# A two-layer decoder step on one core: expert rows scattered to token order, empty slots skipped, other order of the first loads

## The reference, cut to what matters

```
g_idx = argmax(g_logits)                       # one of 4 groups
top_v, top_i = top_k(e_sel, 2)                 # two of its 8 experts
up = t @ w_up[g];  gate, val = split(up)       # 1024 -> 2 x 256
hid = silu(gate) * val * comb
out = out + hid @ w_down[g]                    # 256 -> 1024
x = layer_norm(alpha * x + out)
```

## Time and profile before

| | |
|---|---|
| median of 3 runs | 1686.9 us (1682.15 to 1692.32) |
| profiled execution, its own time | 1689.43 us |
| its span, first to last instruction | 1687.8 us |
| PE busy | 1314.4 us, 78% of the span |
| DVE, ACT, POOL busy | 29%, 24%, 7% |
| granted TensorE clock, mean | 0.849 |
| DMA | 340.30 MB, mean 202 GB/s |

### The profile page before, as it was taken

The page is one execution under the profiler, slowest core; times in us unless marked ns, Lnnn a source line. Parts: engine busy times, 40 slices in busy tenths (PEclk is TensorE's granted clock), DMA queues, the critical chain, the costliest instruction groups (busy, mean ns, idle before and its releaser), DMA issues.

```text
span 1687.8 us, 17971 instructions
## 1 busy us (share of the span) xinstructions
PE 1314.4 (78%) x7094; PEld 899.7 (53%) x7094; DVE 493.2 (29%) x989; ACT 398.0 (24%) x757; POOL 121.5 (7%) x146
## 2 busy tenths in 40 slices
PE   7979997688667877772799999997688496787840
PEld 6979995556432322222799978783466332232310
DVE  2353137544510000006410157314443400000007
ACT  3112221530112222221212146322420022122110
POOL 0200001000000000005200020000000000000013
PEclk9989998698778988885897969797788698898875
DMA  8532214500579999975114040142400879999953
GB/s 317 225 112 75 88 38 140 186 7 32 201 269 414 414 414 415 413 287 192 41 39 155 26 151 1 38 132 87 124 25 25 338 272 414 414 413 415 413 194 109
DMA packets 161794, 340.30 MB, mean 202 GB/s; under 512 B 18610, under 2 KB 53570, under 8 KB 161474
## 3 DMA queue, kind: packets, MB, share of 16 engines
q1 hardware_dynamic: 143698, 274.98, 43.4%
q0 software_dynamic: 13424, 47.65, 7.5%
q10 hardware_dynamic: 4608, 16.78, 2.4%
HBM read 299.57 MB, written 39.81 MB: 201 GB/s over the span
## 4 chain that ended last, share of the span: by engine, by line
PE 55%; DMA 19%; DVE 11%; SPq 9%; ACT 4%; issue 2%; POOL 0%; ACTq 0%; DVEq 0%
DMA weight_ring<-in_w_up_dram 9%; PE ps L671 8%; PE ps L672 8%; PE ps L673 8%; PE ps L860 8%; DMA expert_weights<-in_w_up_dram 6%; SPq L444 6%; SPq L448 3%; PE ps L1132 2%; PE ps L924 2%; PE ps L1154 2%; PE ps L792 2%; PE ps L1200 1%; DVE small L1716 1%; DVE x_rows L1724 1%
## 5 line engine op out<-in xcount | busy, mean ns | idle before, releaser
L860 PE MATMUL ps<-weight_ring,work 128*64 128x512 f32 x512 | 139.5, 706 | 62.0 <-DMA weight_ring<-in_w_up_dram 62.0
L1855 DVE TENSOR_TENSOR work<-ps,work 128x256 f32<-128x256 f32 x32 | 13.6, 424 | 519.3 <-ACT work L1390 519.3
L860 PE MATMUL ps<-expert_weights,work 128*64 128x512 f32 x512 | 135.8, 691 | 34.8 <-DMA expert_weights<-in_w_up_dram 32.3
L860 PEld LDWEIGHTS ps<-weight_ring,work 128*64 128x64 f32 x512 | 47.4, 163 | 153.6 <-issue 153.6
L672 PE MATMUL ps<-weight_ring_r,mix_cols_r 128*128 128x384 f32 (+3 forms) x360 | 121.4, 338 | 0.0
L860 PEld LDWEIGHTS ps<-expert_weights,work 128*64 128x64 f32 x512 | 41.8, 159 | 127.4 <-issue 84.0
L673 PE MATMUL ps<-mix_cols_r,weight_ring_r 128*128 128x272 f32 x352 | 102.4, 291 | 0.0
L1390 ACT ACTIVATE work<-ps 128x256 f32<-128x256 f32 x32 | 12.3, 383 | 260.3 <-PE ps L860 260.3
L546 POOL DMA_INDIRECT work<-stream_rows,ints x34 | 32.0, 943 | 540.4 <-PE ps L841 493.3
L672 PEld LDWEIGHTS ps<-weight_ring_r,mix_cols_r 128*128 128x128 f32 (+1 forms) x360 | 67.4, 187 | 4.2
L671 PE MATMUL ps<-expert_weights_r 128*128 128x512 f32 (+1 forms) x160 | 68.5, 428 | 0.4 <-DVE mix_cols_r L1708 0.4
(11 more groups left out here) (365 smaller groups left out, 2443.5 us busy)
## 6 DMA issues: line engine op xcount, KB each, us to landing
expert_weights<-in_w_up_dram SPq DMA_DIRECT2D x32, 2048.0 KB, 19.8
weight_ring<-in_w_up_dram SPq DMA_DIRECT2D x32, 2048.0 KB, 19.8
expert_weights<-in_w_down_dram SPq DMA_DIRECT2D x32, 1024.0 KB, 16.7
mix_cols<-in_w_down_dram SPq DMA_DIRECT2D x32, 1024.0 KB, 16.0
expert_rows<-work ACTq DMA_DIRECT2D x32, 512.0 KB, 6.6
weight_ring<-in_w_in_a_dram SPq DMA_DIRECT2D x8, 1536.0 KB, 6.5
expert_rows<-expert_weights POOLq DMA_DIRECT2D x16, 512.0 KB, 9.9
weight_ring<-in_w_o_dram SPq DMA_DIRECT2D x4, 2048.0 KB, 13.0
```

What stands on the lines that cost most here:

```text
L860: last = mm(bank(0, rows=(t.start, t.stop)), xgT[:, k, t], WU[2 * q + j][:, k, :], start=(k == 0), stop=(k == KD - 1))
```

## The change

1. **Slots.** Constants `token` and the new `target` are stored minus 4096 (`FAR`); DVE adds 4096 to both lists. A filled slot gets its token and its row `token + 544 j` in the new layout of `expert_rows` (two halves of 544 rows); an empty one gets 4096, which the bounds of gather and scatter leave out. `bb` grows from 64 to 96 columns.
2. **Gather and scatter.** Both are indirect DMAs with a bounds check, issued by POOL. The scatter takes the place of the copy issued by ACT, and stands in POOL's order between two gathers. ACT's loop over pairs is written out.
3. **Combination.** SP loads a tile's two rows by one plain DMA; POOL only adds. In layer 0 `chunk(CH_S)` stands after the rows of tile 0, `chunk(CH_S + 1)` after those of tile 1.
4. **No zero fill** of `expert_rows`, and no wait for it.
5. **First loads.** SP loads input rows, weight chunk 0 and the rotary tables ahead of the other memory chunks; PE forms memory chunks 1 to 3 after heads 2, 5 and 8.
6. Some semaphores are merged into `f_step` and `fs_step`, with the same order of work.

```diff
-        ys_all = nc.dram_tensor("expert_rows", [(PAIRS + MORE) * P, D], F32, kind="Internal").ap()
+        ys = nc.dram_tensor("expert_rows", [2 * TOK, D], F32, kind="Internal").ap()
...
+            def gather(l, tokens, landed):
+                pool.indirect_dma_start(xg, None, xs[l], bass.IndirectOffsetOnAxis(tokens, 0), bounds_check=TOK - 1,
+                                        oob_is_err=False).then_inc(landed, 16)
+
+            def scatter(rows, landed):
+                pool.indirect_dma_start(ys, bass.IndirectOffsetOnAxis(rows, 0), yb, None, bounds_check=2 * TOK - 1,
+                                        oob_is_err=False).then_inc(landed, 16)
...
-                for i in range(PAIRS + 1):
-                    pool.wait_ge(S("xg_free"), b + i + 1)
-                    pool.indirect_dma_start(xg, None, xs[l], bass.IndirectOffsetOnAxis(slot_tok[:, i:i + 1], 0)) \
-                        .then_inc(S("xg_in"), 16)
+                gather(l, slot_tok[:, 0:1], S("xg_in"))
+                for i in range(PAIRS):
+                    pool.wait_ge(S("xg_free"), b + i + 2)
+                    gather(l, slot_tok[:, i + 1:i + 2], S("xg_in"))
+                    pool.wait_ge(S("y_ev"), s + i + 2)
+                    scatter(slot_to[:, i:i + 1], S("y_out"))
...
+            def expert_rows(l, i):
+                if i == 0:
+                    sp.wait_ge(S("y_out"), 16 * PAIRS * (l + 1))
+                    sp.wait_ge(S("rows_done"), l + 1)
+                if i >= 2:
+                    sp.wait_ge(S("yg_used"), NT * l + i - 1)
+                n = ROWS[i]
+                sp.dma_start(yg[i % 2][0:n], ys.rearrange("(j t) d -> t j d", j=2)[P * i:P * i + n]) \
+                    .then_inc(S(f"yg_in{i % 2}"), 16)
...
-                    last = mm(bank(5, 0, 64), a1[:, n, :], bb[:, n, :], start=(n == 0), stop=(n == 9))
+                    last = mm(bank(5, 0, 3 * NE), a1[:, n, :], bb[:, n, :], start=(n == 0), stop=(n == 9))
...
+                if h in (2, 5, 8):
+                    mem_kv_chunk((h + 1) // 3)
             pe.wait_ge(S("mkv_ev"), 8)
+            for l in range(LAYERS):
+                mem_keys_columns(l)
+            pe.wait_ge(S("mkt_ev"), 2)
```

More of the change, by code:

```diff
@@ L327, in build @@
         a1 = view(work, 2530, 10, P)
-        bb = view(work, 3810, 10, 2 * NE)
+        bb = view(work, 3810, 10, 3 * NE)
         esw = view(work, 6976, NT * NG * EG)
@@ L503, in _ @@
             experts(0)
-            sp.wait_ge(S("yg_in0"), 32)
-            for n in range(CH_S, CH_END):
+            expert_rows(0, 0)
+            chunk(CH_S)
+            expert_rows(0, 1)
+            chunk(CH_S + 1)
+            for i in range(2, NT):
+                expert_rows(0, i)
+            for n in range(CH_S + 2, CH_END):
                 chunk(n)
-            sp.wait_ge(S("tables"), 64)
+            sp.wait_ge(S("tables"), 48)
             sp.wait_ge(S("fm_mm"), 10)
@@ L526, in _ @@
             experts(1)
+            for i in range(2):
+                expert_rows(1, i)
+            for i in range(2, NT):
+                expert_rows(1, i)
             for i in range(ST):
@@ L581, in _ @@
-            nc.gpsimd.memset(zeros, 0.0).then_inc(S("pool_zero"), 1)
-            pool.wait_ge(S("pool_zero"), 1)
-            pool.wait_ge(S("rope_mm"), 1)
-            for b in range(MORE):
-                pool.dma_start(ys_all[(PAIRS + b) * P:(PAIRS + b + 1) * P], zeros).then_inc(S("zero_out"), 16)
+                pool.sem_inc(S("rows_done"), 1)
+                for i in range(NT):
+                    pool.wait_ge(S(f"yg_in{i % 2}"), 16 * ((3 if i % 2 == 0 else 2) * l + i // 2 + 1))
+                    y = yg[i % 2][0:ROWS[i]]
+                    nc.gpsimd.tensor_tensor(y[:, 0], y[:, 0], y[:, 1], ALU.add).then_inc(S("yg_sum"), 1)
```

207 lines of the change are left out of this document (98 added, 109 removed).

## The result

The changed kernel takes 1710.2 us (median of 4 runs, 1706.2 to 1716.8), the kernel before 1687.8 (4 runs): a ratio of 1.014, 95% interval 1.010 to 1.018. It is slower by 22 us; the forecast was 1657 and faster. The profiled execution is the longest of the four, 1716.81 us, its span 1715.1.

A forecast was written before the change was run, and what follows sets the result against it. Bytes were taken to bound the expert stages, PE and its DVE/ACT feeders the rest. Terms -20.4, -1.4, +1.2, -5.4, -1.4, -2.6 sum to -30.0 us: 1659.4, or 1657 against the median; 8 in 10 within 1642 to 1679.

The forecast's parts named there:

- The pace of bytes: Expert stages: all DMA engines busy at 414 GB/s, so transfers set the time of a pair, 17.6 us.
- the large term: Expert stages: skipping empty slots saves 2.3 rows a transfer on the fullest engine, 10.2 us a layer, -20.4 us (0 to -33).
- the even end: Expert stages: empty rows spread evenly over engines, 3.75 rows saved a transfer, 16.6 us a layer; as a rival 1644 us, 21%.
- the sign that should tell: Expert stages: DMA share stays near 1.04 if all engines lose rows, falls below 1 if the fullest sets the pace.
- Scatter on POOL between gathers: Expert stages: POOL waits for a pair's copied result and scatters before issuing the next gather; cost 0.
- the right ring: Expert stages: up product's end to result 7.3 us, scatter and gap, gather landing 6.9 us; 15.4 us in all.
- Its cover: Expert stages: turning wants the gather at about 16.9 us, leaving 1.5 us spare, then PE's wait for weights, about 3 us.
- The rival on the slower side: Expert stages: POOL becomes the bound if scatter and gather each take 5 us; about 1713 us, 6% with the like.
- Start: Before the experts: no zero fill delays chunk 2, less low clock, some new waits; -5.4 us (-12 to +2).
- Routing: Ahead of the first gather in both layers: a third part of `bb` and one more list; +1.2 us (0 to +2.5).
- First gather: Start of each expert stage: fewer rows per engine land it sooner; -1.4 us in both layers (0 to -6).
- Combination: After the experts: scatter and plain load replace copy and gathers; -1.4 us in layer 1, -2.6 in layer 0.

The follow-up runs named there:

- e3: The kernel before, plus a wait on POOL for pair i's copied result before the gather of pair i+2; 1688.2 us, ratio 0.999.
- e4: The kernel before, with only the gathers skipping empty slots (bounds check, `xg` zeroed once a layer), copies unchanged; 1674.1 us, ratio 0.991.
- e8: The kernel before, with the sixteen zero fills issued later, after the first projected rows of the second phase; 1676.9 us, ratio 0.992.
- e1: The changed kernel, with POOL issuing the gather of pair i+2 before the wait for pair i's result and the scatter; 1674.0 us, ratio 0.991.
- e6: The changed kernel with the gather issued ahead of wait and scatter, and no row skipped; 1698.0 us, ratio 1.005.
- e5: e1 with the slots of an expert dealt evenly over the partitions; 1665.3 us, ratio 0.982.
- e9: e5, without zero fill, with first loads and memory products in the order of the kernel before; 1654.9 us, ratio 0.981.
- e10: e6, but the scatter writes the pair's own block of rows, one behind the other; 1695.4 us, ratio 1.004.
- e14: e10 with a plain DMA issued by POOL in place of the indirect scatter; 1698.3 us, ratio 1.005.
- e2: The changed kernel, order on POOL kept, but no row skipped: empty slots move real or spare rows; 1742.2 us, ratio 1.031.

## Why the prediction was wrong

**The pace of bytes and the large term: right.** Bytes set the pace before (e3, e4, e8 keep the waits for weights). The term was 10.2 us a layer, 2.3 rows a transfer. Read alone (e1 against e6) it is 10.7 and 13.0, 2.4 and 2.9 rows. Dealt evenly (e5 against e6) it is 16.4 and 16.3, the even end of 16.6. The figure worked out from the Trainium skill, "DMA: Bandwidth & Descriptors", section "The descriptor swizzle", was 15.5 for both layers; 23.7 were measured, so these transfers save more than it gives. The pair of 17.0 us did not come all the same: behind the two short intervals e1's pairs take 17.8 and 17.6 us, those of the kernel before 17.8, since the copy's new queue (below) takes back what the rows give. What was wrong is the sign that should tell: the DMA share stayed at 1.01 to 1.04 in all kernels but e9 (0.99), so it tells neither who is full nor whether bytes are the bound.

**Scatter on POOL between gathers, cost 0: this step failed.** The prediction had the right wait and the right queue, and its 15.4 us are the right ring, once around for one pair: turning, down product and result (7.3), scatter and gap (1.24), landing of the gather (6.9). Two things were wrong with it.

Its length: 18.7 us were measured where PE waits for the gather, 3.3 more. 1.8 of them lie between turning and copy (7.7 instead of 5.9 us), at the lower clock that follows PE's wait; 0.8 between copy and gather issue; 0.7 in the landing, which has the scatter ahead of it.

Its cover: the ring was compared with the 16.9 us of a pair at the pace of weights, and PE's wait for weights, 3 us, was lent as further cover. But those 16.9 us contain this wait already. A ring longer than the pace costs the whole difference in every pair. e3 shows the ring without the scatter at 16.4 us, under the 17.6 of the weights: no cost. The changed kernel shows it at 18.7: the scatter's issue (1.35 us), the slower turning (0.7) and the later landing (0.3).

The order costs 20.3 and 17.4 us (after against e1), 37.7 together, where 0 was forecast. The rival on the slower side had the right place and 1713 us, and came near the time by luck. It put the turning and the down product into the ring twice, took it for two pairs (29.7 us, "14.9 a pair"), and so needed 5 us for each of scatter and gather; they take 1.01.

**The same copy on another queue: missing.** That ACT loses the issue and POOL takes it was booked as nothing for the transfers. The expert stages of e6, e10 and e14 are 9 to 10 us longer than the mean of before, e3 and e8 (8 against before alone), with the same bytes; that it is the queue is argued by elimination.

**Start: right in size and parts.** -5.4 forecast, -4.5 in the trace (-3.4 to -6.1 in the kernels with this start); two small misses cancel in part. The fill cost 12.7 (12.0 forecast) and the order 8.1, of which 5.3 and 0.7 (keys; 1.3 forecast) were named; where the other 2 us went was not followed. At the end of the kernel the gain is lost among the differences between runs.

**Routing: half of what it cost.** From the rank products to the first gather's issue: 15.69 us before, 16.85 after, +1.16 in layer 0 alone, and +1.31 in layer 1; +1.2 was forecast for both together. The +0.4 ahead of the ten products came as forecast; behind them 0.75 were added and not 0.2, and e4, with one list and no third part of `bb`, already has 0.6 of it. **First gather: no gain.** PE waits 9.11 and 9.04 us instead of 8.31 and 8.11, but most of that is the routing behind the ten products. From the gather's issue to the turning it is 7.69 and 7.46 us instead of 7.58 and 7.37; -1.4 for both was forecast. e4, which skips rows in the form of the kernel before, has 7.29 and 7.25, and e2 and e6, the new form with all rows, 7.65 to 7.73. So skipping brings 0.1 to 0.3, and something in the new form costs as much; it wasn't followed further.

**Combination: right, and better than forecast.** Layer 1, in the timeline of the changed kernel:

```profile
1662.46 1.00 POOL L563 DMA_INDIRECT expert_rows<-work,ints  x1 [10.16 <-ACT work L1419]
1665.83 0.37 SPq L487 DMA_DIRECT2D work<-expert_rows  x1
...
1671.27 2.33 POOL L602 TENSOR_TENSOR work<-work 128x1024 f32<-128x1024 f32 x1 [7.82 <-DMA work<-expert_rows]
```

8.8 us instead of 11.6, -2.8 for -1.4: the scatter lands in 3.4 us, not 5.1. The later tiles win another 3.3, since POOL's gather issues no longer stand among its additions; the prediction had counted nothing for them. Layer 0: from the last down product to the split of the chunk 19.0 us instead of 23.9, -4.9 for -2.6; the split then takes 5.57 instead of 3.43 beside POOL's addition.

The sum as it should have read, in stages measured against e6 and e1: rows -23.7, the copy's new queue +16 to +19, order +37.7, start -4.5, routing and first gather +2.7, combinations about -8: +20 to +23. The medians differ by 22.3, the two profiled executions by 27.3. This is a division of the measured change and no second proof of it: the first three terms are differences along one chain (before, e6, e1, after) and must add up to the change in the stages. The rest up to 27.3 lies mostly in parts whose code is equal.

## What to carry to other kernels

Before you move a wait, close the ring: follow the waiting engine's next instruction until it comes back to the same one, count by how many tiles it has advanced, and compare its length per tile with the present pace; a cover that is itself a wait is none. An instruction that needs a late result goes behind those that need only early ones on its queue. Count the low clock behind the new wait as part of the ring. A second bound can stand close below the first: here 16.4 us (e3's ring) beside 17.6, so a saving and a small delay in one change can end as a loss.

## What was not expected of the hardware

- With the pair's 512 KB result issued by POOL and not by ACT, indirect or plain, scattered or not, a pair took 0.55 us more (17.8 against 17.3 us, 398 against 411 GB/s: e6, e10, e14 against e3 and before). That it is the queue is argued, not shown.
- A row outside the bounds of an indirect DMA still leaves a packet, of under 512 B: 144 packets per transfer in either case, 4.1% instead of 7.5% of the engines' time (e4 against e3).
- An issue with bounds check takes 1.01 us in the changed kernel and 0.99 in e4, against 0.94 without; the check of 128 rows costs at most 0.07 us.
- The same turning takes 1.09 us or 1.97, depending on the clock that PE is granted after its wait (1.00 and 0.50, both in e3).
- DVE's split of a chunk takes 5.57 us beside an addition on POOL (3.43 without one), and the addition 3.43 instead of 2.33:

```profile
797.77 3.43 POOL L602 TENSOR_TENSOR expert_weights<-expert_weights 128x1024 f32<-128x1024 f32 x1 [4.44 <-DMA expert_weights<-expert_rows]
798.91 5.57 DVE L1723 TENSOR_TENSOR weight_ring_r<-weight_ring,weight_ring_r 128x1536 fp32r<-128x1536 f32 x2
```
